# Second block's projections as ten chunk pairs of seven products, weight sums on GpSimd, convolution begun with two chunks

## The chip, the cores and the metric

One core of one Trainium2 chip runs the whole kernel. The metric is the device time of one execution in microseconds; less is better. All data is float32. In the code and the profile TensorE is PE (PEld its weight loads), VectorE is DVE, ScalarE is ACT, GpSimd is POOL and SyncE is SP.

## The reference

The program computes two transformer-like blocks one after the other on 512 tokens of 1024 features. The change touches only the second block, which puts 16 meta tokens ahead (528 tokens) and has two layers. Each layer begins with one wide projection, out of which come queries, keys, values, a gated depthwise convolution and two gates:

```
u = h @ w_in[i]                       # 528 x 1024 times 1024 x 3840
q = u[..., :512]                      # 8 heads of 64
k = u[..., 512:640]                   # 2 heads of 64
v = u[..., 640:768]
y_attn = sliding_window_attention(q, k, v, ...) @ w_attn_proj[i]
y_conv = conformer_conv(u[..., 768:1792], ...) @ w_conv_proj[i]
mix = (sigmoid(u[..., 1792:2816]) * y_attn + sigmoid(u[..., 2816:]) * y_conv) @ w_out[i]

def conformer_conv(u, dw, db, g, b):  # 31 taps, causal, per channel
    val, gate = split(u, 2)
    h = val * sigmoid(gate)
    return silu(layer_norm(depthwise_conv(h, dw) + db, g, b))
```

## The kernel before, in words

The features of a layer lie transposed in `core.feat` (128 partitions x 8 x 528 tokens). The projection's output is made in chunks of 128 output features: 4 of the convolution's value, 4 of its gate, 4 of queries, 2 of keys, 1 of values (token by token, not feature by feature), 16 of gates. The host lays the weights out in that order (`lay_out`). Each key head of 64 features is laid out twice in its chunk, since PE's score matmuls need the key on the same partitions as the query, either 0 to 63 or 64 to 127.

`project_and_attend` (L2351) is one block in which each engine has its own program, in an order written out by hand; semaphores tie them together.

- SP loads the weights in groups of up to four chunks (`GROUPS`, L2108), 2 MB each, alternately into `core.lead` and `w`. Groups 0 and 1 are there before layer 0's stage starts; in layer 1 group 1 is issued at its start. `load_behind(g, semaphore, count)` (L2434) issues group g when the named work has been done.
- PE: a chunk is made in two halves of 264 tokens, each by 8 matmuls into one of two PSUM banks (`ring`), by `chunk_half` (L2460). It makes the 28 halves of value, gate, queries and keys, then the values (L2530), then the first 14 halves of the gates (`EARLY`), and then waits for the convolution (`own`, `CONVOLVED` = 124 instructions). After that come the column sums of the convolution's result (L2481), the scores and the attention, unit by unit, with the other 18 gate halves placed between (two halves directly behind the first scores).
- ACT moves each half out of its bank (`take`, L2563 to L2565), through a sigmoid for the convolution's gate.
- DVE multiplies value and gate (L2648) of all four chunks, then runs the convolution: two iterations, each with 31 taps for two chunks of 528 tokens (L2660 for the first tap, L2663 for the others: source and result in SBUF, the weight a column). Each instruction waits for the one two places before it. Then it centres the result (L2671) once PE has the column sums.
- POOL clears the padding of the gated input (L2450) and then does nothing until the softmax (L2456).

The two layers of the block run this function with the same code; in layer 0 the attention has two small units for the meta tokens more. The dense feed-forward part of layer 0 (`dense_ffn`, L2848) already multiplies in pairs of chunks by seven products (L2947), with the sums on DVE.

Of the kernel before, what the change touches and what calls it, by code (L numbers as in the profile page):

```python
# [2107 lines left out]
GROUPS = [(0, 4), (4, 4), (8, 4), (12, 3), (15, 4), (19, 4), (23, 4), (27, 4)]  # L2108
# [242 lines left out]
def project_and_attend(core, A, i, weights, mix_in):  # L2351


    units = []
# [9 lines left out]
    PLAIN = 14  # L2364
# [3 lines left out]
    first_gate = PLAIN * 2  # L2368
    CONVOLVED = CCK * CW
    with ExitStack() as ctx:  # L2370
# [9 lines left out]
        ring = core.ps(ctx, "ring", [P, RINGS, BANK])  # L2380
        ps = core.ps(ctx, "ps", [P, 2, BANK])
        pm = core.ps(ctx, "pm", [P, 2, BANK])
        ptr = core.ps(ctx, "ptr", [P, BANK])
        po = core.ps(ctx, "po", [P, BANK])
# [3 lines left out]
             "t_out o_made o_out centred squared rooted inverse normed silu").split())  # L2388
        ident, ones = core.cst[:, ID0:ID0 + P], core.cst[:, ONE0:ONE0 + P]
        eps = core.cols2[:, LAYERS * C2L:LAYERS * C2L + 1]  # L2390
        tap0 = i * C2L
        SUMS = first_gate + EARLY
# [11 lines left out]

        def gate_half(h):

            return first_gate + h + (0 if h < EARLY else 2 if h < EARLY + 2 else 4)
# [18 lines left out]
        with core.block() as block:  # L2426

            @block.sync
            def _(sp):
                if i == 0:  # L2430
                    core.tables.load(sp)
                if i:
                    weights.first_loads(sp, (1,))
                def load_behind(g, done, count):  # L2434
                    sp.wait_ge(done, count)
                    weights.load(sp, g % 2, *GROUPS[g])

# [11 lines left out]
            def _(pool):  # L2449
                pool.memset(glu[:, :, 0:CW - 1], 0.0).then_inc(padded, 1)  # L2450
# [8 lines left out]
            def _(pe):  # L2459
                def chunk_half(n, g, c, half, part=None):  # L2460
# [3 lines left out]
                    for k in ks:  # L2464
                        last = pe.matmul(ring[:, n % RINGS, 0:HALF], w[g % 2][:, c, k * P:(k + 1) * P], core.feat[:, k, cols(half)],  # L2465
                                         start=k == 0, stop=k == DK - 1)
# [3 lines left out]
                def gate(h, part=None):  # L2470
                    g, c = 4 + h // 8, h // 2 % 4
                    if h % 8 == 0 and not part:
                        pe.wait_ge(w_landed[g % 2], 16 * (g // 2 + 1))
                    chunk_half(gate_half(h), g, c, h % 2, part)

                def column_sums(n0, src):
                    for half in range(2):
                        n = n0 + half
                        pe.wait_ge(taken, n - RINGS + 1)
# [4 lines left out]
                def scores(u):  # L2484
# [4 lines left out]
                    for j in range(G):  # L2489
# [3 lines left out]
                        last = pe.matmul(meta(u)[:, b, c, :], q, core.k_t[rows, hk, 0:META], start=True, stop=True)  # L2493
                        if width:
                            last = pe.matmul(main(u)[:, b, c, 2 * P - width:], q, core.k_t[rows, hk, lo - width:lo], start=True, stop=True)
# [26 lines left out]
                for g in range(4):  # L2522
                    pe.wait_ge(w_landed[g % 2], 16 * (g // 2 + 1))
                    for c in range(4 if g < 3 else 2):
                        for half in range(2):
                            n = (g * 4 + c) * 2 + half
                            chunk_half(n, g, c, half)
                for t, r in ROWS:
                    for k in range(DK):
                        last = pe.matmul(ps[0:r, t // 4, (t % 4) * P:(t % 4 + 1) * P], core.feat[:, k, row_cols(t)],  # L2530
                                         w[1][:, 2, k * P:(k + 1) * P], start=k == 0, stop=k == DK - 1)
                last.then_inc(v_made, 1)
# [29 lines left out]
            def _(act):  # L2562
                def take(n, dst, f, half):  # L2563
                    act.wait_ge(projected, n + 1)
                    act.activation(dst[:, cols(half)], ring[:, n % RINGS, 0:HALF], f).then_inc(taken, 1)  # L2565

                def gate(h):
                    if h // 2 >= 2 * DK - CCK - 1:
                        act.wait_ge(normed, CCK)
                    take(gate_half(h), core.gates[:, h // 2, :], ACT.Copy, h % 2)  # L2570
# [11 lines left out]
                act.wait_ge(padded, 1)  # L2582
                for n in range(first_gate):
                    c, half = divmod(n, 2)
                    if c < 4:
                        take(n, val[:, c, :], ACT.Copy, half)
                    elif c < 8:
                        take(n, glu[:, c - 4, CW - 1:], ACT.Sigmoid, half)
                    elif c < 12:
                        take(n, core.q_t[:, c - 8, :], ACT.Copy, half)  # L2590
                    else:
                        take(n, core.k_t[:, c - 12, :], ACT.Copy, half)
                act.wait_ge(v_made, 1)
                act.activation(core.v_tok[:, 0:4, :].rearrange("p t c -> p (t c)"), ps[:, 0, :], ACT.Copy)
                act.activation(core.v_tok[0:META, 4, :], ps[0:META, 1, 0:P], ACT.Copy).then_inc(v_out, 1)
                for h in range(EARLY):
                    gate(h)
                act.wait_ge(centred, CCK)
                act.wait_ge(taken, SUMS)
# [1082 lines left out]
def lay_out(inputs):  # L3682
# [7 lines left out]
    ks = [w2[:, :, q1 + h * HD:q1 + (h + 1) * HD] for h in range(KVH)]  # L3690
    w2 = np.concatenate([w2[:, :, v1:v1 + 2 * CC], w2[:, :, 0:q1], ks[0], ks[0], ks[1], ks[1], w2[:, :, k1:v1],
                         w2[:, :, v1 + 2 * CC:]], axis=2)
# [67 lines left out]
```

## Time and profile before

| | us |
|---|---|
| median of 3 runs (lowest, highest) | 3172.27 (3168.92, 3183.77) |
| the profiled execution's own time | 3173.29 |
| its span | 3171.5 |
| PE busy | 2946.1 (93%) |
| DVE busy | 1131.1 (36%) |
| ACT busy | 567.5 (18%) |
| POOL busy | 221.1 (7%) |
| mean granted clock of PE, of full speed | 0.961 |

The span is the time from the first to the last instruction in one profiled execution. Busy times of engines overlap, so they do not add up to the span. A matmul's record (its mean is printed in ns) is longer than the distance between two matmuls, since they are pipelined; the rate of a stretch is best read from two starts with the number of records between them. Each matmul of the code on float32 data is two records.

### The profile page before, as it was taken

The numbers are of one execution on the slowest core, as the hardware profiler recorded it, in microseconds if no ns is written. First come the engines' busy times: TensorE is split into PE (matmuls) and PEld (weight loads), VectorE is DVE, ScalarE is ACT, GpSimd is POOL, SyncE is SP. The second block draws the span as 40 slices with busy tenths as digits, with TensorE's granted clock in tenths as the row PEclk, the third lists the DMA queues.
The fourth block names the chain that finished last, engine by engine and source line by source line (L and its number), as shares of the span: only waits on it lengthen the run. The fifth ranks groups of instructions, "written<-read, shape, count | busy, mean of one in ns | idle before, by whom it ended". The sixth has DMA issues, their size and how long they took to land. (4 is left out here: it accounts for less than half of the span.)

```text
span 3171.5 us, 43527 instructions
## 1 busy us (share of the span) xinstructions
PE 2946.1 (93%) x18242; PEld 1809.0 (57%) x18242; DVE 1131.1 (36%) x2071; ACT 567.5 (18%) x1340; POOL 221.1 (7%) x204
## 2 busy tenths in 40 slices
PE   8998799999969979999999999999999799999897
PEld 4544788654433327876668874478775444444343
DVE  5666666563132132922343320229212211111014
ACT  3232333222111121134011110011340000000001
POOL 0000332340000000001100000000110100000001
PEclk9999799999969988999999999999999799999998
DMA  3411000107089942212032212022020724547917
GB/s 117 103 59 44 3 17 17 54 14 277 32 339 430 423 200 64 76 58 80 41 126 80 88 71 87 0 73 103 31 95 1 278 74 181 235 181 322 416 44 290
DMA packets 79329, 414.20 MB, mean 131 GB/s; under 512 B 10515, under 2 KB 16019, under 8 KB 63428
## 3 DMA queue, kind: packets, MB, share of 16 engines
q1 hardware_dynamic: 67868, 384.75, 30.6%
q10 hardware_dynamic: 7848, 14.61, 1.9%
q0 software_dynamic: 3456, 12.58, 1.1%
q8 instruction: 118, 1.93, 0.3%
q14 instruction: 39, 0.32, 0.0%
HBM read 383.17 MB, written 28.76 MB: 130 GB/s over the span
## 5 line engine op out<-in xcount | busy, mean ns | idle before, releaser
L3469 PE MATMUL pgu<-gu,xg 128*64 128x320 f32 (+1 forms) x2560 | 393.8, 463 | 10.3 <-POOLq L3397 10.3
L3469 PEld LDWEIGHTS pgu<-gu,xg 128*64 128x64 f32 x2560 | 182.4, 137 | 206.3 <-issue 131.6
L312 PE MATMUL proj<-feat,w 128*128 128x512 f32 x576 | 256.1, 598 | 2.5 <-PEq L153 2.5
L2465 PE MATMUL ring<-feat,lead 128*128 128x264 f32 x1024 | 242.6, 397 | 3.0 <-PEq L3069 1.5
L2465 PEld LDWEIGHTS ring<-feat,lead 128*128 128x128 f32 x1024 | 197.6, 196 | 40.4 <-issue 6.3
L2465 PE MATMUL ring<-feat,w 128*128 128x264 f32 x896 | 209.4, 390 | 0.0
L3476 PE MATMUL py<-down,hm_t 128*64 128x512 f32 x880 | 199.0, 600 | 10.4 <-POOLq L3397 10.4
L2465 PEld LDWEIGHTS ring<-feat,w 128*128 128x128 f32 x896 | 169.1, 192 | 30.3 <-issue 2.4
L312 PEld LDWEIGHTS proj<-feat,w 128*128 128x128 f32 x576 | 107.3, 191 | 124.8 <-issue 124.8
L497 DVE SCALAR_TENSOR_TENSOR mixed<-padded,taps,mixed 128x512 f32<-128x512 f32 x216 | 162.4, 752 | 7.7
L2663 DVE SCALAR_TENSOR_TENSOR conv<-vg,cols,conv x240 | 163.4, 769 | 0.0
L3089 PE MATMUL po<-wd,hm 128*128 128x512 f32 x352 | 152.2, 593 | 0.0
L3538 DVE TENSOR_TENSOR hm<-sg,pgu 128x384 f32<-128x384 f32 (+1 forms) x40 | 20.8, 521 | 314.9 <-PE pgu L3469 209.5
L3476 PEld LDWEIGHTS py<-down,hm_t 128*64 128x64 f32 x880 | 61.7, 138 | 121.0 <-issue 103.8
L3089 PEld LDWEIGHTS po<-wd,hm 128*128 128x128 f32 x352 | 66.5, 190 | 83.5 <-issue 83.5
L2778 PE MATMUL pp<-wo,feat 128*128 128x512 f32 x256 | 111.3, 593 | 2.8 <-POOL feat L2827 2.8
L3421 ACT ACT_TABLE_LOAD x19 | 24.4, 1283 | 459.7 <-PE pgu L3469 280.9
L3035 DVE TENSOR_TENSOR gb<-gb,pp 128x264 f32<-128x264 f32 x66 | 28.2, 429 | 174.8 <-PE pp L2947 174.8
L2778 PEld LDWEIGHTS pp<-wo,feat 128*128 128x128 f32 x256 | 48.1, 190 | 61.9 <-issue 61.9
L2947 PE MATMUL pp<-sums_x,sums_w 128*128 128x264 f32 x352 | 80.1, 386 | 0.0
L2947 PEld LDWEIGHTS pp<-sums_x,sums_w 128*128 128x128 f32 x352 | 66.9, 190 | 11.4
L2219 ACT ACTIVATE rt<-rt 128x1 f32<-128x1 f32 (+1 forms) x15 | 3.0, 203 | 376.7 <-DVE rt L2189 376.7
(521 smaller groups left out, 3952.1 us busy)
## 6 DMA issues: line engine op xcount, KB each, us to landing
gu<-in_moe_gu SPq DMA_DIRECT2D x16, 3072.0 KB, 13.5
gu<-in_moe_gu SPq DMA_DIRECT2D x16, 2560.0 KB, 15.9
ring<-in_w_gate SPq DMA_DIRECT2D x16, 2048.0 KB, 13.6
ring<-in_w_up SPq DMA_DIRECT2D x16, 2048.0 KB, 15.2
ring<-in_w_down SPq DMA_DIRECT2D x16, 2048.0 KB, 17.5
w<-in_w_in SPq DMA_DIRECT2D x15, 2048.0 KB, 7.8
down<-in_moe_down SPq DMA_DIRECT2D x8, 3072.0 KB
down<-in_moe_down SPq DMA_DIRECT2D x8, 2560.0 KB, 20.8
```

Of the source, the lines that this page charges most:

```text
L312: last = pe.matmul(proj[:, n % 2, :], w[:, g % 2, k, c * P:(c + 1) * P], core.feat[:, k, :], start=k == 0, stop=k == DK - 1)
L497: dve.scalar_tensor_tensor(out=out, in0=src[:, j:j + SEQ], scalar=taps[:, n, j:j + 1], in1=out, op0=ALU.mult, op1=ALU.add).then_inc(convol ...
L2465: last = pe.matmul(ring[:, n % RINGS, 0:HALF], w[g % 2][:, c, k * P:(k + 1) * P], core.feat[:, k, cols(half)], start=k == 0, stop=k == DK - 1)
L2663: dve.scalar_tensor_tensor(out=out, in0=src[:, j:j + NTOK], scalar=tap(c, j), in1=out, op0=ALU.mult, op1=ALU.add).then_inc(own, 1)
L2778: last = pe.matmul(pp[:, n % 2, n // 2 % 2, 0, :], mixed[:, k, row_cols(t)], wo[:, k, half * BANK:(half + 1) * BANK], start=k == 0, stop=k ...
L2947: last = pe.matmul(bank, lhs[:, a, k * P:(k + 1) * P], rhs[:, k, :], start=begin and k == 0, stop=k == KH - 1, skip_group_check=True)
L3035: dve.tensor_tensor(dst, dst, bank, ALU.add).then_inc(added, 1)
L3089: last = pe.matmul(po[:, t, :], hm[:, f, row_cols(t)], wd[half][:, f, :], start=f == 0, stop=f == FC - 1)
L3421: act.activation(sg[:, q, 0:n], pgu[:, 2 * q, 0:n], ACT.Silu).then_inc(silu, 1)
L3469: last = pe.matmul(pgu[half(h), part, 0:n], xg[:, k, :], w[:, k, h, :], start=k == 0, stop=k == DK - 1)
L3476: last = pe.matmul(py[half(h), :], hm_t[:, c, :], down[:, c, h * BANK:(h + 1) * BANK], start=c == 0, stop=c == XC - 1)
L3538: dve.tensor_tensor(hm[:, c0:c0 + n], sg[:, q, 0:n], pgu[:, 2 * q + 1, 0:n], ALU.mult).then_inc(multiplied, 1)
```

## The change

Strassen's method, in the form of seven products, is used on pairs of chunks. A pair's output (2 x 128 features by 2 x 264 tokens) is a 2 x 2 block product: weights of the two chunks and two halves of the 1024 input features, times the two halves of the features and of the tokens. Instead of 8 products of 4 matmuls each it takes 7, with sums of weight blocks (four per pair, on POOL) and of feature blocks (four per layer, on DVE). The products accumulate in three PSUM banks a pair; ACT copies each bank out before the next product goes onto it, some of them into tiles where they are kept, and POOL adds the kept ones to the result (three adds of 264 columns a pair). The ten pairs are: value 0 and 1, gate 0 and 1, value 2 and 3, gate 2 and 3 (of the convolution), two pairs of queries, one pair of the keys with the first chunk of the gates, and three pairs of gates. The keys take one chunk instead of two; PE swaps its two halves of 64 partitions by an identity matmul for the second copy. The values follow pair 6. The 14 early gate halves of before are now in the pairs; the other 18 stay where they were, in layer 1 without the meta tokens (256 columns instead of 264). DVE begins the convolution of chunks 0 and 1 as soon as these two are there, and does the gating of each iteration at its start. The loads stand behind the pairs.

```diff
-GROUPS = [(0, 4), (4, 4), (8, 4), (12, 3), (15, 4), (19, 4), (23, 4), (27, 4)]
+GROUPS = [(0, 4), (4, 4), (8, 4), (12, 3), (15, 4), (19, 4), (23, 4), (27, 3)]
...
+    KH = DK // 2
+    (P1, P2, P6, P5, P7, P3, P4) = range(7)
+    PRODUCTS = 7
+    ADDED = 3
+    PAIR_AT = [(0, 0), (1, 0), (0, 2), (1, 2), (2, 0), (2, 2), (3, 0), (4, 0), (4, 2), (5, 0)]
+    PAIRS2 = len(PAIR_AT)
+    GLU_PAIRS = (1, 3)
+    KEY_PAIR = 6
...
+        def gate_cols(half):
+            return slice(META + half * (SEQ // 2), META + (half + 1) * (SEQ // 2)) if i else cols(half)
...
-                load_behind(2, projected, 8)
-                load_behind(3, projected, 16)
-                load_behind(4, projected, 24)
+                load_behind(2, product, 3 * PRODUCTS)
+                load_behind(3, product, 4 * PRODUCTS)
+                load_behind(4, product, 6 * PRODUCTS)
                 load_behind(5, v_made, 1)
-                load_behind(6, projected, gate_half(7) + 1)
+                load_behind(6, product, 9 * PRODUCTS)
...
-                load_behind(7, projected, gate_half(15) + 1)
+                load_behind(7, projected, gate_half(17) + 1)
 
             @block.gpsimd
             def _(pool):
+                def sum_weights(r):
+                    g, c = PAIR_AT[r]
+                    pool.wait_ge(w_landed[g % 2], 16 * (g // 2 + 1))
+                    if r >= 2:
+                        pool.wait_ge(product, PRODUCTS * (r - 2) + P3 + 1)
+                    for n, (out, x, y, f) in enumerate(((s1(r), weight(r, 1, 0), weight(r, 1, 1), ALU.add),
+                                                        (s2(r), s1(r), weight(r, 0, 0), ALU.subtract),
+                                                        (s3(r), weight(r, 0, 0), weight(r, 1, 0), ALU.subtract),
+                                                        (s4(r), weight(r, 0, 1), s2(r), ALU.subtract))):
+                        if n:
+                            pool.wait_ge(w_summed, 4 * r + n)
+                        pool.tensor_tensor(out, x, y, f).then_inc(w_summed, 1)
+
+                def add(r, dst, n, have):
+                    pool.wait_ge(copied, PRODUCTS * r + have + 1)
+                    pool.tensor_tensor(dst, dst, kept(r, n), ALU.add).then_inc(added, 1)
+
+                sum_weights(0)
                 pool.memset(glu[:, :, 0:CW - 1], 0.0).then_inc(padded, 1)
+                sum_weights(1)
                 core.clear_retired(pool)
+                for r in range(PAIRS2):
+                    add(r, row(r, 0)[:, 0:HALF], 0, P2)
+                    add(r, row(r, 1)[:, HALF:], 2, P7)
+                    add(r, row(r, 0)[:, HALF:], 1, P3)
+                    if r + 2 < PAIRS2:
+                        sum_weights(r + 2)
...
+                def multiply(r, bank, lhs, rhs, begin):
+                    for k in range(KH):
+                        last = pe.matmul(bank, lhs[:, k * P:(k + 1) * P], rhs[:, k, :], start=begin and k == 0,
+                                         stop=k == KH - 1, skip_group_check=True)
+                    last.then_inc(product, 1)
+
+                def pair(r):
+                    g, c = PAIR_AT[r]
+                    pe.wait_ge(w_landed[g % 2], 16 * (g // 2 + 1))
+                    if r >= 2:
+                        pe.wait_ge(copied, PRODUCTS * (r - 2) + P4 + 1)
+                    multiply(r, bank_x(r), weight(r, 0, 0), x11, True)
+                    multiply(r, bank_y(r), weight(r, 0, 1), x21, True)
+                    pe.wait_ge(w_summed, 4 * r + 2)
+                    pe.wait_ge(x_summed, 2)
+                    pe.wait_ge(copied, PRODUCTS * r + P1 + 1)
+                    multiply(r, bank_x(r), s2(r), t2, False)
+                    multiply(r, bank_z(r), s1(r), t1, True)
+                    pe.wait_ge(w_summed, 4 * r + 4)
+                    pe.wait_ge(x_summed, 4)
+                    pe.wait_ge(copied, PRODUCTS * r + P6 + 1)
+                    multiply(r, bank_x(r), s3(r), t3, False)
+                    pe.wait_ge(copied, PRODUCTS * r + P5 + 1)
+                    multiply(r, bank_z(r), s4(r), x22, False)
+                    pe.wait_ge(copied, PRODUCTS * r + P7 + 1)
+                    multiply(r, bank_x(r), weight(r, 1, 1), t4, False)
...
+                def swap_keys():
+                    pe.wait_ge(added, ADDED * (KEY_PAIR + 1))
+                    for half, bank in enumerate((bank_y(PAIRS2), bank_z(PAIRS2))):
+                        for b in range(2):
+                            last = pe.matmul(bank[b * HD:(b + 1) * HD, :], ident[:, (1 - b) * HD:(2 - b) * HD],
+                                             core.k_t[:, 0, cols(half)], start=True, stop=True)
+                        last.then_inc(swapped, 1)
...
-                for h in range(EARLY):
-                    gate(h)
+                for r in range(PAIRS2):
+                    pair(r)
+                    if r == KEY_PAIR:
+                        values()
+                swap_keys()
                 pe.wait_ge(own, CONVOLVED)
                 column_sums(SUMS, core.conv)
                 pe.wait_ge(v_out, 1)
+                pe.wait_ge(k_out, 2)
                 scores(0)
...
+                def open_sums(r):
+                    act.wait_ge(added, ADDED * (r + 1))
+                    act.activation(row(r, 0), row(r, 0), ACT.Sigmoid).then_inc(opened, 1)
+                    act.activation(row(r, 1)[:, HALF:], row(r, 1)[:, HALF:], ACT.Sigmoid).then_inc(opened, 1)
+
+                def pair(r):
+                    if r >= 2:
+                        act.wait_ge(added, ADDED * (r - 1))
+                    copy(r, P1, kept(r, 0), bank_x(r))
+                    copy(r, P2, row(r, 0)[:, 0:HALF], bank_y(r))
+                    copy(r, P6, kept(r, 1), bank_x(r))
+                    copy(r, P5, kept(r, 2), bank_z(r))
+                    if r - 1 in GLU_PAIRS:
+                        open_sums(r - 1)
+                    copy(r, P7, row(r, 1)[:, HALF:], bank_x(r))
+                    copy(r, P3, row(r, 0)[:, HALF:], bank_z(r))
+                    copy(r, P4, row(r, 1)[:, 0:HALF], bank_x(r), ACT.Sigmoid if r in GLU_PAIRS else ACT.Copy)
...
             @block.vector
             def _(dve):
-                for c in range(CCK):
-                    dve.wait_ge(taken, 2 * (4 + c) + 2)
-                    g = glu[:, c, CW - 1:]
-                    dve.tensor_tensor(g, g, val[:, c, :], ALU.mult).then_inc(gated, 1)
-                dve.wait_ge(gated, CCK)
+                for n, (out, x, y) in enumerate(((t1, x12, x11), (t2, x22, t1), (t3, x22, x12), (t4, x21, t2))):
+                    if n:
+                        dve.wait_ge(x_summed, n)
+                    dve.tensor_tensor(out, x, y, ALU.subtract).then_inc(x_summed, 1)
+                dve.wait_ge(padded, 1)
                 if i == 0:
                     dve.wait_ge(core.tables.columns_in, 16)
                 with dve.Fori(0, CCK // 2) as r:
                     done = r * (2 * CW)
+                    dve.wait_ge(opened, r * 2 + 2)
+                    for e in range(2):
+                        c = r * 2 + e
+                        g = glu[:, bass.ds(c, 1), CW - 1:].rearrange("p a n -> p (a n)")
+                        v = val[:, bass.ds(c, 1), :].rearrange("p a n -> p (a n)")
+                        dve.tensor_tensor(g, g, v, ALU.mult).then_inc(gated, 1)
+                    dve.wait_ge(gated, r * 2 + 2)
                     for j in range(CW):
```

## Rows read from the trace of the kernel before

**Rows 1.** The page's first part: busy time, share and instructions of each engine.

```profile
PE 2946.1 (93%) x18242; PEld 1809.0 (57%) x18242; DVE 1131.1 (36%) x2071; ACT 567.5 (18%) x1340; POOL 221.1 (7%) x204
```

**Rows 2.** Instructions in order of time, layer 0, PE: start, us, work, count.

```profile
1201.22 31.53 PE L2465 MATMUL ring<-feat,lead 128*128 128x264 f32 x128 [1.48 <-PEq L2253]
1232.58 28.64 PE L2465 MATMUL ring<-feat,w 128*128 128x264 f32 x128
1261.06 28.64 PE L2465 MATMUL ring<-feat,lead 128*128 128x264 f32 x128
...
1303.78 9.16 PE L2530 MATMUL ps<-w,feat 128*128 128x128 f32 x80
...
1362.81 3.72 PE L2481 MATMUL ring<-conv,cst 128*128 128x264 f32 x16
```

**Rows 3.** The same for layer 1.

```profile
2068.57 31.34 PE L2465 MATMUL ring<-feat,lead 128*128 128x264 f32 x128 [1.48 <-PEq L3069]
...
2229.98 3.72 PE L2481 MATMUL ring<-conv,cst 128*128 128x264 f32 x16
```

**Rows 4.** Busy time by stretch of 20 us: PE, PEld, DVE, ACT, POOL, granted clock, DMA.

```profile
1201.00:1221.00 20.00, 19.78 (x76) 16.51 (x77) 0.00 (x0) 1.56 (x4) 0.20 (x1) 0.85 0.27 68
```

**Rows 5.** Instructions in order of time, layer 0, DVE.

```profile
1261.68 0.71 DVE L2648 TENSOR_TENSOR vg<-vg 128x528 f32<-128x528 f32 x1 [6.41 <-ACT vg L2565]
1262.92 1.02 DVE L2660 TENSOR_SCALAR conv<-vg,cols  x2 [0.53 <-DVE vg L2648]
...
1304.71 1.02 DVE L2660 TENSOR_SCALAR conv<-vg,cols  x2
1305.64 40.84 DVE L2663 SCALAR_TENSOR_TENSOR conv<-vg,cols,conv  x60
1364.88 1.45 DVE L2671 SCALAR_TENSOR_TENSOR conv<-ring,conv 128x264 f32<-128x264 f32 x4 [18.39 <-PE ring L2481]
```

**Rows 6.** Groups of instructions by line and form, ACT: count, busy us, mean ns.

```profile
L2565 ACT ACTIVATE vg<-ring 128x264 f32<-128x264 f32 x32 | 12.5, 391 | 106.3 <-PE ring L2465 106.3
L2789 ACT ACTIVATE gates<-gates 128x528 f32<-128x528 f32 x16 | 8.6, 628 | 0.0
```

**Rows 7.** DMA issues from 2040 to 2260: KB each, us to landing; SP's first.

```profile
w<-in_w_in SPq DMA_DIRECT2D x3, 2048.0 KB, 7.8
```

**Rows 8.** Groups by line and form, POOL.

```profile
L2827 POOL TENSOR_TENSOR feat<-gates 128x528 f32<-128x528 f32 x8 | 10.4, 1300 | 62.9 <-DVE gates L2803 62.9
L2827 POOL TENSOR_TENSOR feat<-gates 128x512 f32<-128x512 f32 x8 | 10.1, 1267 | 61.4 <-DVE gates L2803 61.4
```

**Rows 9.** In order of time, first block: DVE alone, DVE beside POOL, POOL then, POOL alone.

```profile
597.83 1.29 DVE L1568 TENSOR_TENSOR steps_and_weighted<-cst,scal 128x512 f32<-128x512 f32 x2
...
672.18 2.97 DVE L1568 TENSOR_TENSOR steps_and_weighted<-cst,scal 128x512 f32<-128x512 f32 x2
...
668.77 5.83 POOL L1321 TENSOR_TENSOR steps_and_weighted<-tok_x,scal 128x512 f32<-128x512 f32 x4
...
656.62 1.04 POOL L1328 TENSOR_TENSOR state<-state,scal 128x512 f32<-128x512 f32 x1
```

**Rows 10.** DVE and POOL together earlier, and L1027's durations (min/median/max).

```profile
322.51 4.42 DVE L1027 TENSOR_TENSOR uc<-am,shapes 32x256 f32<-32x256 f32 x4
...
322.56 1.51 POOL L678 TENSOR_TENSOR qm<-qm,chan 128x512 f32<-128x512 f32 x1
...
L1027 DVE TENSOR_TENSOR uc<-am,shapes x32: 403/423/1404, 322.5 to 530.3; 32x256 f32<-32x256 f32 x32
```

**Rows 11.** DVE with an input in PSUM, beside a POOL instruction.

```profile
656.01 0.68 DVE L1599 TENSOR_TENSOR hid<-pi,scal 128x512 f32<-128x512 f32 x1
...
655.38 1.28 POOL L1337 TENSOR_TENSOR chan<-chan,hid 128x512 f32<-128x512 f32 x1 [0.59 <-issue]
```

**Rows 12.** PE in order of time: the same work behind a wait and without one.

```profile
2260.19 2.17 PE L2518 MATMUL po<-pt,v_tok 16*64 16x256 f32 x8 [4.41 <-ACT pt L2627]
...
1404.14 1.23 PE L2518 MATMUL po<-pt,v_tok 16*64 16x256 f32 x8
```

More of the change, by code:

```diff
@@ L2363, in project_and_attend @@
     scale = HD ** -0.5
-    PLAIN = 14
     RINGS = 2
@@ L2388, in project_and_attend @@
              "t_out o_made o_out centred squared rooted inverse normed silu").split())
+        product, copied, added, opened, w_summed, x_summed, swapped, k_out = (
+            core.sem(x) for x in "product copied added opened w_summed x_summed swapped k_out".split())
+        x11, x12 = core.feat[:, 0:KH, 0:HALF], core.feat[:, 0:KH, HALF:]
+        x21, x22 = core.feat[:, KH:, 0:HALF], core.feat[:, KH:, HALF:]
+        t1, t2, t3, t4 = (sums_x[:, n, :, :] for n in range(4))
         ident, ones = core.cst[:, ID0:ID0 + P], core.cst[:, ONE0:ONE0 + P]
@@ new lines, in values @@
+                def values():
+                    for t, r in ROWS:
+                        for k in range(DK):
+                            last = pe.matmul(ps[0:r, t // 4, (t % 4) * P:(t % 4 + 1) * P], core.feat[:, k, row_cols(t)],
+                                             w[1][:, 2, k * P:(k + 1) * P], start=k == 0, stop=k == DK - 1)
+                    last.then_inc(v_made, 1)
+                def swap_keys():
[5 more added lines that the diff above has]
+                        last.then_inc(swapped, 1)
@@ L2464, in chunk_half @@
                     for k in ks:
-                        last = pe.matmul(ring[:, n % RINGS, 0:HALF], w[g % 2][:, c, k * P:(k + 1) * P], core.feat[:, k, cols(half)],
+                        src = core.feat[:, k, gate_cols(half)]
+                        last = pe.matmul(ring[:, n % RINGS, 0:src.shape[1]], w[g % 2][:, c, k * P:(k + 1) * P], src,
                                          start=k == 0, stop=k == DK - 1)
@@ L2470, in gate @@
                 def gate(h, part=None):
-                    g, c = 4 + h // 8, h // 2 % 4
-                    if h % 8 == 0 and not part:
+                    g, c = gate_at(h)
+                    if c == 0 and h % 2 == 0 and not part:
                         pe.wait_ge(w_landed[g % 2], 16 * (g // 2 + 1))
@@ L2478, in column_sums @@
                         n = n0 + half
-                        pe.wait_ge(taken, n - RINGS + 1)
+                        if n >= RINGS:
+                            pe.wait_ge(taken, n - RINGS + 1)
+                        elif half:
+                            pe.wait_ge(copied, PRODUCTS * PAIRS2)
                         for c in range(CCK):
@@ L2492, in scores @@
                         q = core.q_t[rows, hk * 2 + c, q0:q0 + nq]
-                        last = pe.matmul(meta(u)[:, b, c, :], q, core.k_t[rows, hk, 0:META], start=True, stop=True)
+                        last = pe.matmul(meta(u)[:, b, c, :], q, core.k_t[rows, abs(b - hk), 0:META], start=True, stop=True)
                         if width:
-                            last = pe.matmul(main(u)[:, b, c, 2 * P - width:], q, core.k_t[rows, hk, lo - width:lo], start=True, stop=True)
+                            last = pe.matmul(main(u)[:, b, c, 2 * P - width:], q, core.k_t[rows, abs(b - hk), lo - width:lo], start=True, stop=True)
                     last.then_inc(s_made, 1)
@@ L2562, in _, with copy @@
             def _(act):
-                def take(n, dst, f, half):
-                    act.wait_ge(projected, n + 1)
-                    act.activation(dst[:, cols(half)], ring[:, n % RINGS, 0:HALF], f).then_inc(taken, 1)
+                def copy(r, j, dst, bank, f=ACT.Copy):
+                    act.wait_ge(product, PRODUCTS * r + j + 1)
+                    act.activation(dst, bank, f).then_inc(copied, 1)
+                def open_sums(r):
[14 more added lines that the diff above has]
+                    copy(r, P4, row(r, 1)[:, 0:HALF], bank_x(r), ACT.Sigmoid if r in GLU_PAIRS else ACT.Copy)
                 def gate(h):
@@ L2569, in gate @@
                         act.wait_ge(normed, CCK)
-                    take(gate_half(h), core.gates[:, h // 2, :], ACT.Copy, h % 2)
+                    n = gate_half(h)
+                    dst = core.gates[:, h // 2, gate_cols(h % 2)]
+                    act.wait_ge(projected, n + 1)
+                    act.activation(dst, ring[:, n % RINGS, 0:dst.shape[1]], ACT.Copy).then_inc(taken, 1)
                 def soft(u):
@@ L2580, in soft @@
                     act.activation(x[:, 1, :], x[:, 1, :], ACT.Exp).then_inc(exped, 1)
[L2582 to L2597, printed above, removed]
+                for r in range(PAIRS2):
+                    pair(r)
+                    if r == KEY_PAIR:
+                        act.wait_ge(v_made, 1)
+                        act.activation(core.v_tok[:, 0:4, :].rearrange("p t c -> p (t c)"), ps[:, 0, :], ACT.Copy)
+                        act.activation(core.v_tok[0:META, 4, :], ps[0:META, 1, 0:P], ACT.Copy).then_inc(v_out, 1)
+                for half, bank in enumerate((bank_y(PAIRS2), bank_z(PAIRS2))):
+                    act.wait_ge(swapped, half + 1)
+                    act.activation(core.k_t[:, 1, cols(half)], bank, ACT.Copy).then_inc(k_out, 1)
                 act.wait_ge(centred, CCK)
-                act.wait_ge(taken, SUMS)
                 act.sem_inc(taken, 1)
```

57 lines of the change are left out of this document (35 added, 22 removed).

## The prediction

> **What bounds the kernel now.** I read the page first: TensorE (PE) is busy 93% of the span, so anything that takes matmuls away looks like gain [rows 1]. That share is an average; the change touches two stages, the projections of the two layers of the second block, so I then read PE in order of time there [rows 2]. In layer 0 the stage starts at 1201.22 and runs without a gap (28 ring halves, the values, 14 gate halves) to the column sums at 1362.81: 161.6 us. I call the start T=0. Layer 1 is a copy: 2068.57 to 2229.98, 161.4 us [rows 3]. In steady state 128 records of 128x264 take 28.48 us from start to start, 0.2225 us each (each matmul of the code is two records); the first 128 take 31.36, that is 2.9 us more, with a granted clock of 0.85 in the first 20 us [rows 2, 4]. The values cost 9.1 us.
>
> The column sums wait for the convolution on VectorE (DVE), the chain of 124 dependent instructions, so I read DVE in the same stretch [rows 5]. Four gatings come as the ring gives them, the convolution starts at 1262.92 (T=61.7), each of its two iterations takes 41.8 us (1262.92 to 1304.71), and it ends at 1346.5, T=145.3. Then DVE is idle 18.4 us until PE's column sums. So PE sets the end now, and the convolution has 16.3 us of slack. Two paths run side by side: what the change is worth is the later of the two afterwards.
>
> **PE's path.** Before the sums: 336 matmuls of ring halves (42 x 8) and the values. After: 10 pairs x 7 products x 4 = 280, the values, and 4 for the swapped keys. In records: 560 x 0.2225 = 124.6, plus 9.1, plus 8 x 0.2225 = 1.8, plus the 2.9 of the slow start: PE arrives at T=138.5 instead of 161.6, 23.1 us earlier. The parts I cost at nothing on it: ScalarE's copies, 0.39 us each [rows 6], lie under the next product of 8 x 0.2225 = 1.8 us, since each bank is reused only one product later; where the two sigmoids (0.63 for 528 columns and 0.39 for 264) come between two copies, the copy of P7 ends about 1.3 us late, still under P3. The one load of an activation table falls on the last copy of pair 1, which PE needs only a pair later. Weight loads land in 7.8 us [rows 7]; the tightest is group 2, issued behind pair 2 and needed a pair (12.46 us) later; layer 1's group 1 is issued at its start (2068.5, SyncE is free then) and its sums are needed at about T=19. SyncE's queue has only the layer-0 tables and these loads in it. The last group is issued behind gate half 17 instead of 15 and used from half 26 instead of 24. The DVE sums of the inputs (four of 1056 elements, estimated at 1.3 us each from 0.71 for 528 [rows 5]) must be half done at about T=6.5 and all done at T=10: close, up to 1 us.
>
> **GpSimd (POOL).** Per pair, 4 sums of 128x512 and 3 adds of 128x264. An addition with two full inputs takes 1.27 us for 512 and 1.30 for 528 [rows 8]; by that slope (2.06 ns an element) 264 take 0.76. That is 7.4 us of 12.46 per pair: POOL keeps up, and even if each instruction is held up by 0.35 us (half a DVE instruction) it has 2.5 us left. It works one pair ahead, so PE waits for no sum. In POOL's queue the sums of pair 4 stand ahead of the adds of pair 3; with the load landing at T=48.1 they end near 54.5, and the adds are through at 57.8, before pair 4's sigmoids need them at about 60.
>
> **The convolution's path.** Pairs 0 and 1 end at T=27.8; after P1, P2, P6 and P5 of pair 2 (7.1 us) and a copy the two sigmoids run, and DVE starts at T=36.6. A gating and the step to the convolution cost 1.24 us and a second gating 0.71, 1.95 together; an iteration 41.8; the second iteration's inputs are long there: 36.6 + 2 x 43.75 = T 124.1, if nothing slows DVE. That would be 14 us before PE.
>
> But before the change POOL is silent here, and now it reads and writes SBUF all the time. In the first block the trace has this pair of engines side by side. While POOL runs four additions back to back (5.83 us for 4), DVE's additions with both inputs in SBUF take 2.97 us for two; two of the same line without POOL take 1.29 [rows 9]. So in steady alternation one DVE and one POOL instruction share 1.45 us: DVE loses 0.8 us for each POOL instruction, which alone takes 1.04 (its second input is broadcast). Where POOL's two inputs are full, as here, four DVE instructions of 32x256 take 4.42 us, 1.1 each, where the median is 0.42 and the largest is 1.40: a loss of up to 0.98 for each POOL instruction, whose own records grow from 1.27 to 1.51 [rows 10]. A DVE instruction with one input in PSUM is not slowed beside POOL (0.68) [rows 11]. The convolution's instruction reads its source and its accumulator from SBUF, so it is of the first kind; that scalar_tensor_tensor behaves like tensor_tensor is my choice, no row shows it.
>
> Nearest to the new case are the full inputs of [rows 10]. I take 0.95 us for a sum and 0.48 for an add (half the elements). Under the convolution lie the sums of pairs 4 to 9 (24) and the last 2 adds of pair 2 with those of pairs 3 to 9 (23): 22.8 + 11.0 = 33.8 us. The convolution ends at T=157.9, and the column sums start at 158.1 instead of 161.6. Ends of this cost: nothing at all; the smallest slot that the trace shows, 0.7 and 0.35 (25 us); POOL's whole record each time, 1.28 and 0.76 (48.2 us).
>
> The Trainium skill (page "SBUF — State Buffer", section "Who interferes with whom") says that a DVE instruction with two SBUF inputs contends with a GpSimd instruction that reads SBUF, and that whoever comes second waits for the whole instruction. That speaks against this change. The trace agrees on which instructions collide, but an alternation takes 1.45 us where the whole-instruction reading gives 0.64 + 1.02 = 1.66; by the page's wording the sum would be that of the second rival.
>
> PE then stands idle from T=138.5 to 158.1. After such a gap it is slow: behind 4.4 us of waiting the row of 8 records at 2260.19 takes 2.17 us instead of 1.23 [rows 12], and the start of the stage costs 2.9 us. I take 2.9 again. What follows the sums (scores, 18 gate halves, attention) is unchanged, except that in layer 1 the gate halves have 256 columns for 264: 288 records x 0.2225 x 8/264 = 1.9 us less.
>
> **Sum.** Per layer 158.1 + 2.9 - 161.6 = -0.6 us; two layers -1.2; gates -1.9: -3.1 us. The profiled execution took 3173.29 (span 3171.5), so 3170.2 by its time; the median of the three runs is 3172.27, 1.0 lower, which gives 3169.
>
> **Rivals.**
> 1. DVE loses little, because the dependent chain leaves POOL room between instructions (0.681 us apart where two free additions come 0.60 to 0.65 apart). With no loss PE sets the end at T=138.5: 2 x 23.1 + 1.9 = 48 us less, 3124. With the small slots (25 us lost) the convolution ends at 149.1: 2 x 9.4 + 1.9 = 21 less, 3152. For it: no row shows this form of instruction beside POOL. Against it: every DVE row with two SBUF inputs beside POOL is slowed.
> 2. Slower: POOL's whole record blocks DVE each time. Loss 48.2, convolution ends at T=172.3: 2 x (172.5 + 2.9 - 161.6) - 1.9 = +26, 3198. It decides from a loss of about 35 us a layer on (break even), and is over 0.5% slower from 43.3. For it: the 1.40 of [rows 10], where a 0.42 instruction lost 0.98. Against it: the 1.45 of the alternation.
> 3. POOL falls behind: were each of its instructions to wait a whole DVE instruction (0.68), it would need 4 x 2.0 + 3 x 1.5 = 12.7 us a pair against PE's 12.46. PE would arrive up to 2 us later, hidden behind the convolution: 3169 again.
>
> **How the numbers follow.** Forecast 0.56, with a range of its own of 3157 to 3184 (a loss of 28 to 41 us a layer); rival 1 0.26; rival 2 0.14; rival 3 0.04. A measurement of this kernel can tell 0.5%, 16 us. Faster by more than that needs a loss below 27.4 us: rival 1 and the edge of the forecast, 0.28. Slower: rival 2, 0.14. The rest, 0.58, is no change. The range takes in most of rival 1 and half the way to rival 2: 3136 to 3188.
>
> **What would show it.** In the changed trace: PE's last product before the values and after pair 9 near T=137, then a gap of some 20 us before the column sums, ended by DVE's convolution; the mean of the convolution's instruction well above 0.769 us, its two iterations 55 to 60 us instead of 41.8; POOL's sums at 1.4 to 1.6 us instead of 1.27; a granted clock under 1 at the column sums. I am wrong if the convolution's instruction stays near 0.77 and the column sums follow PE's last product without a gap, or if the gap is over 28 us, or if PE waits inside the pairs for sums or copies.

## The result and the profile after

The changed kernel takes 3196.85 us (median of 7, 3193.4 to 3198.0) where the kernel before takes 3169.1 (median of 7 beside it, 3165.65 to 3183.77). The medians stand 27.8 us apart; the ratio taken over the executions is 1.0073, with a 95% interval of 1.0061 to 1.0085. It is slower by 0.7%, clear of the noise. The forecast was 3169, no change. T counts from PE's first matmul of the stage, and everything is set against the rows of before.

The busy times of the page after, and PE in order of time: layer 0, then layer 1.

```profile
PE 2908.3 (91%) x18034; PEld 1772.3 (55%) x18034; DVE 1192.7 (37%) x2079; ACT 593.3 (19%) x1408; POOL 454.0 (14%) x344
```

```profile
1199.55 5.41 PE L2542 MATMUL pp<-feat,lead 128*128 128x264 f32 x16 [1.48 <-PEq L2253]
...
1251.53 3.72 PE L2542 MATMUL pp<-feat,lead 128*128 128x264 f32 x16
1282.26 6.72 PE L2542 MATMUL pp<-sums_x,sums_w 128*128 128x264 f32 x16 [27.01 <-POOL sums_w L2516]
...
1344.17 6.48 PE L2542 MATMUL pp<-sums_x,sums_w 128*128 128x264 f32 x16 [12.18 <-POOL sums_w L2516]
...
1381.89 3.83 PE L2607 MATMUL pp<-conv,cst 128*128 128x264 f32 x16
...
2091.64 6.49 PE L2542 MATMUL pp<-feat,lead 128*128 128x264 f32 x16 [1.48 <-PEq L3208]
...
2228.55 1.11 PE L2578 MATMUL pp<-k_t,cst 128*64 128x264 f32 x8
2250.02 5.83 PE L2607 MATMUL pp<-conv,cst 128*128 128x264 f32 x16 [20.35 <-DVE conv L2802]
```

The two layers run the same code and went two ways. In layer 1 PE has made its swapped keys and is at the wait at T=138.0 (2250.02 - 20.35 - 2091.64), and waits 20.35 us for DVE; the column sums start at T=158.4, where before they started at 161.4 [rows 3]. In layer 0 PE waits inside the pairs, 27.01 us in pair 4 and 12.18 in pair 7, both times for POOL's sums, and the column sums start at T=182.3 instead of 161.6 [rows 2]. To the first matmul of the mixing behind it (1510.92 after, 1489.66 before), layer 0 grew by 22.9 us, counted from PE's start; layer 1 (2370.29, 2348.47) shrank by 1.3. The span grew by 23.7 us, 21.6 of it in these two stretches.

POOL in order of time, layer 0 and layer 1:

```profile
1247.04 33.83 POOL L2516 TENSOR_TENSOR sums_w<-lead 128x512 f32<-128x512 f32 x1 [8.34 <-DMA lead<-in_w_in]
1280.94 1.26 POOL L2516 TENSOR_TENSOR sums_w<-sums_w,lead 128x512 f32<-128x512 f32 x1
...
1315.88 26.90 POOL L2516 TENSOR_TENSOR sums_w<-lead 128x512 f32<-128x512 f32 x1 [9.43 <-DMA lead<-in_w_in]
...
2139.64 5.71 POOL L2516 TENSOR_TENSOR sums_w<-lead 128x512 f32<-128x512 f32 x1 [8.21 <-DMA lead<-in_w_in]
2145.43 1.62 POOL L2516 TENSOR_TENSOR sums_w<-sums_w,lead 128x512 f32<-128x512 f32 x1
2147.13 1.61 POOL L2516 TENSOR_TENSOR lead<-lead 128x512 f32<-128x512 f32 x1
```

and DVE in the same stretches (the rows of 60 are the taps of one iteration):

```profile
1237.45 1.54 DVE L2799 TENSOR_SCALAR conv<-vg,cols  x2 [0.68 <-DVE vg L2791]
1238.91 40.83 DVE L2802 SCALAR_TENSOR_TENSOR conv<-vg,cols,conv  x60
1290.50 2.48 DVE L2791 TENSOR_TENSOR vg<-vg  x2 [10.75 <-ACT vg L2689]
...
1294.76 46.90 DVE L2802 SCALAR_TENSOR_TENSOR conv<-vg,cols,conv  x60
...
2129.80 1.03 DVE L2799 TENSOR_SCALAR conv<-vg,cols  x2 [0.32 <-DVE vg L2791]
2130.76 67.89 DVE L2802 SCALAR_TENSOR_TENSOR conv<-vg,cols,conv  x60
...
2201.61 48.36 DVE L2802 SCALAR_TENSOR_TENSOR conv<-vg,cols,conv  x60
```

One addition of 128x512, 1.27 us before [rows 8], has a record of 33.83 us; I call such an instruction held. It ends 1.1 us behind the end of the first iteration (1238.91 + 40.83 = 1279.74), and that iteration runs at its old speed of 40.83 us [rows 5] as if POOL were not there. Between the iterations POOL comes in; in the second one the next first sum behind a load is held for 26.90 us, until 1342.78, again 1.1 us behind the chain's end (1294.76 + 46.90). In layer 1 the addition is held for 5.71 us, and from then on POOL and DVE take turns, so that the iteration takes 67.89 us.

Behind such waits PE is slow: granted clock 0.53 in the wait of pair 4 and 0.50, the level of 1.2 GHz, in the 6 us after it (per stretch: PE, PEld, DVE, ACT, POOL, clock, DMA). The 16 records behind the two waits take 6.72 and 6.48 us, where others of the same form take 3.72.

```profile
1256.00:1282.00 26.00, 0.00 (x0) 0.00 (x0) 23.74 (x35) 0.00 (x0) 25.92 (x2) 0.53 0.06 26
1282.00:1288.00 6.00, 5.74 (x13) 4.51 (x14) 0.00 (x0) 0.39 (x1) 5.84 (x7) 0.50 0.00 0
```

### The profile page after: what moved, and what is told of

It reads as the page before. It is cut to its first block and busy times, and to the rows that moved or that the text cites. A ratio compares the mean times of both kernels' runs of the same rounds, so it can differ in the third digit from the quotient of the medians.

```text
span 3195.2 us, 43423 instructions
## 1 busy us (share of the span) xinstructions
PE 2908.3 (91%) x18034; PEld 1772.3 (55%) x18034; DVE 1192.7 (37%) x2079; ACT 593.3 (19%) x1408; POOL 454.0 (14%) x344
## 5 line engine op out<-in xcount | busy, mean ns | idle before, releaser
L3608 PEld LDWEIGHTS pgu<-gu,xg 128*64 128x64 f32 x2560 | 182.3, 137 | 206.3 <-issue 131.8
L2802 DVE SCALAR_TENSOR_TENSOR conv<-vg,cols,conv x240 | 204.0, 925 | 0.0
L2516 POOL TENSOR_TENSOR sums_w<-lead 128x512 f32<-128x512 f32 x12 | 78.9, 6573 | 693.0 <-POOLq L3208 520.8
L2542 PE MATMUL pp<-sums_x,sums_w 128*128 128x264 f32 x320 | 80.2, 407 | 39.2 <-POOL sums_w L2516 39.2
L3545 POOL DMA_INDIRECT gu<-moe_out,place x8 | 8.1, 1016 | 641.7 <-POOLq L3541 639.6
L2588 PE MATMUL pp<-feat,w 128*128 128x264 f32 (+1 forms) x320 | 80.6, 401 | 0.0
L3086 PE MATMUL pp<-sums_x,sums_w 128*128 128x264 f32 x352 | 80.1, 386 | 0.0
```

The costliest lines, as they stand in the source:

```text
L2516: pool.tensor_tensor(out, x, y, f).then_inc(w_summed, 1)
L2542: last = pe.matmul(bank, lhs[:, k * P:(k + 1) * P], rhs[:, k, :], start=begin and k == 0, stop=k == KH - 1, skip_group_check=True)
L2588: last = pe.matmul(ring[:, n % RINGS, 0:src.shape[1]], w[g % 2][:, c, k * P:(k + 1) * P], src, start=k == 0, stop=k == DK - 1)
L2802: dve.scalar_tensor_tensor(out=out, in0=src[:, j:j + NTOK], scalar=tap(c, j), in1=out, op0=ALU.mult, op1=ALU.add).then_inc(own, 1)
L3086: last = pe.matmul(bank, lhs[:, a, k * P:(k + 1) * P], rhs[:, k, :], start=begin and k == 0, stop=k == KH - 1, skip_group_check=True)
L3608: last = pe.matmul(pgu[half(h), part, 0:n], xg[:, k, :], w[:, k, h, :], start=k == 0, stop=k == DK - 1)
```

## The experiments

Theory A: a chain of DVE instructions with no gap keeps a port to SBUF that it shares with POOL; a POOL instruction that needs this port and comes when the chain has run undisturbed for a while waits until the chain breaks. Rival B: the long records wait for the weight load in front of them (the rows of both name a DMA). Rival C: POOL's own long pause makes it slow. The runs show which instructions are held beside which; that a port is the reason is the theory's part.

**The chain by itself.** This is no part of the kernel: 40 dependent instructions like the convolution's a trial, and one piece of POOL work after a set number of them (steps). In a chain two apart, as the convolution is, each instruction waits for the one two places before it; one apart, for the one directly before it.

```diff
+ dve.wait_ge(own, at + (j - apart + 1))
+ dve.scalar_tensor_tensor(out=out, in0=src[:, j:j + W], scalar=one[:, j:j + 1], in1=out, ...).then_inc(own, 1)
...
+ pool.wait_ge(own, start + s)
+ pool.tensor_tensor(wo[:, 0, 0:size], wa[:, 0:size], wb[:, 0:size], ALU.add).then_inc(done, 1)
```

> Not the kernel: DVE's convolution chain by itself (40 dependent instructions of 128x528 a trial, each waiting for the one two places before), and in each trial one POOL instruction that comes after 4 to 20 steps of the chain; POOL has been idle until then, or busy with memsets; it is an addition of 512 or 264 elements, a copy or a memset. Then six trials with the chain one apart and six with it four apart. Theory A (a chain in undisturbed rhythm keeps the shared SBUF port; an addition that comes after a long calm waits for the chain's end): additions that come after 8 or more calm steps last until the chain ends (10 to 20 us), those after 4 to 6 steps about 1.2 to 1.8 us; memsets 0.5 us at any place; with the chain one apart, where a gap lies between two instructions, none is over 2 us. Rival B (the long instructions of layer 0 waited for the weight load, not for the port): no instruction here is over 2 us, since there is no load. Rival C (a long idle time makes POOL slow, not DVE's rhythm): the additions with memsets ahead of them are short, those without are long at the same step.

POOL's records, in order: an addition after 6 steps; 12 memsets and the addition behind them, at step 12; a copy after 12; a memset after 12; an addition after 5; and with the chain one apart an addition after 8 and four after 20.

```profile
38.58 24.13 POOL L73 TENSOR_TENSOR wo<-wa,wb 128x512 f32<-128x512 f32 x1 [27.56 <-DVE acc L94]
...
201.95 6.92 POOL L61 MEMSET wm<- 128x512 f32 x12 [0.82 <-DVE acc L91]
208.84 19.98 POOL L73 TENSOR_TENSOR wo<-wa,wb 128x512 f32<-128x512 f32 x1
...
345.83 19.43 POOL L69 COPY wo<-wa 128x512 f32<-128x512 f32 x1 [7.61 <-DVE acc L94]
...
399.88 0.52 POOL L71 MEMSET wo<- 128x512 f32 x1 [7.60 <-DVE acc L94]
...
512.37 1.72 POOL L73 TENSOR_TENSOR wo<-wa,wb 128x512 f32<-128x512 f32 x1 [2.87 <-DVE acc L94]
...
654.15 1.26 POOL L73 TENSOR_TENSOR wo<-wa,wb 128x512 f32<-128x512 f32 x1 [6.00 <-DVE acc L94]
...
828.78 6.31 POOL L73 TENSOR_TENSOR wo<-wa,wb 128x512 f32<-128x512 f32 x4 [38.27 <-DVE acc L94]
```

All 10 lone additions of 512 that came after 6 to 20 steps lasted to the end of the chain, 14.62 to 24.13 us, also those of 264 after 12 and 20 (19.54, 14.10) and the copies; those after 4 and 5 steps took 1.72. Additions are held with no load in the program, so B is not needed; 12 memsets directly ahead change nothing (19.98 where an idle POOL had 20.06), so C is refuted; no memset was held. With the chain one apart nothing is held; four apart it is held as two apart (22.77). I had expected an addition after 6 steps to be short, and it was held.

> The chain by itself again, POOL idle before one addition of 512 elements a trial. 14 trials come after 2 to 8 steps, each twice: by the first such run (1.7 us after 4 and 5 steps, 24 us after 6) the additions after up to 5 steps take under 2 us and those after 6 or more last to the chain's end, both times. Then chains of another kind, with the addition after 10, 13, 17 and 20 steps. Chain of instructions with one input in SBUF: if the shared read port is what is kept, none is over 2 us; if any dense chain shuts POOL out, they last 14 to 20 us. Chain of tensor_tensor with two inputs: held like the convolution's. A gap every 8 steps: the addition waits at most 8 x 0.68 = 5.4 us and takes at most 7; a gap every 16 steps: at most 10.9 + 1.3 = 12.2 us.

The edit is in the list of trials, `s` from 2 to 8 and the forms of the chain. POOL's records: after 5 steps, after 6, a chain of instructions with one SBUF input, a gap every 8 steps, a gap every 16.

```profile
93.73 1.72 POOL L61 TENSOR_TENSOR wo<-wa,wb 128x512 f32<-128x512 f32 x1 [26.88 <-DVE acc L87]
122.33 24.13 POOL L61 TENSOR_TENSOR wo<-wa,wb 128x512 f32<-128x512 f32 x1 [26.88 <-DVE acc L87]
...
401.11 14.99 POOL L61 TENSOR_TENSOR wo<-wa,wb 128x512 f32<-128x512 f32 x1 [4.56 <-DVE acc L82]
...
582.70 1.72 POOL L61 TENSOR_TENSOR wo<-wa,wb 128x512 f32<-128x512 f32 x1 [6.39 <-DVE acc L87]
...
696.37 5.12 POOL L61 TENSOR_TENSOR wo<-wa,wb 128x512 f32<-128x512 f32 x1 [19.79 <-DVE acc L87]
```

Both passes give the same: up to 5 instructions since the chain's start 1.72 us, from 6 on held to the end. A gap every 8 leaves 1.72 in all four trials, one every 16 gives 5.12, 3.08, 1.72, 1.72. A chain of tensor_scalar from SBUF to SBUF holds POOL too (14.99 to 10.34 us), like one of tensor_tensor (19.61 to 13.42). So a second SBUF tensor as input is not needed. But this form steps every 0.47 us where tensor_tensor steps every 0.62, so it may read in another way, and the trial does not tell which port is kept. Why the sixth instruction decides here is open too, and it is no rule for the kernel: with four pairs (below), an add of 264 elements that came 4.6 us behind POOL's last turn, with seven of the convolution's instructions started between, took 0.96 us.

**Sums as memsets.** It leaves out POOL's sums and adds and puts memsets in their place, so the block's values are meaningless and only the projection stages are read.

```diff
-                        pool.tensor_tensor(out, x, y, f).then_inc(w_summed, 1)
+                        write_only(w_summed, idle[:, 0:2 * BANK])
-                    pool.tensor_tensor(dst, dst, kept(r, n), ALU.add).then_inc(added, 1)
+                    write_only(added, idle[:, 0:2 * HALF])
```

> POOL's sums of weights and its adds are left out and memsets of 1024 and 528 elements stand in their place (write only, about 0.95 and 0.5 us), every wait kept; the second block computes something else, so only its projection stages are read, not its total. Theory A (port): no POOL instruction over 1.2 us, both iterations of the convolution 41.8 to 42.5 us in both layers, PE has no wait inside the pairs, and the column sums start at T = 138 to 141 in both layers (182.3 and 158.4 in the changed kernel). Rival B (late load): one POOL instruction behind each load of group 2 and 4 in layer 0 is still 27 to 34 us, and PE waits as long; column sums in layer 0 at T = 165 or more.

POOL behind the load of group 2, the first iteration, and PE's column sums in layer 0:

```profile
1246.83 10.75 POOL L2513 MEMSET pt<- 128x1024 f32 x12 [8.82 <-DMA lead<-in_w_in]
```

```profile
1238.22 40.83 DVE L2815 SCALAR_TENSOR_TENSOR conv<-vg,cols,conv  x60
...
1281.63 40.83 DVE L2815 SCALAR_TENSOR_TENSOR conv<-vg,cols,conv  x60
```

```profile
1336.15 3.83 PE L2620 MATMUL pp<-conv,cst 128*128 128x264 f32 x16
```

The load lands at the same place, nothing is held, both iterations keep 40.83 us, and PE's column sums start 136.5 us after its start at 1199.70, a little ahead of the 138 to 141 expected. So the load does not hold POOL, and layer 0's loss comes from POOL instructions that read SBUF.

**A gap at every fourth tap.**

```diff
-                                dve.wait_ge(own, done + (2 * j + e - 1))
+                                dve.wait_ge(own, done + (2 * j + e - (0 if j % 4 == 0 and e == 0 else 1)))
```

> One edit: at every fourth tap the first of the two chunks' instructions waits for the one directly before it, so that a gap of about 0.1 us stands in the chain 7 times an iteration. Theory A (port kept by the rhythm): a POOL addition waits for at most the next gap, so none is over 7 us; layer 0 becomes like layer 1: column sums at T = 156 to 163 in both (182.3 and 158.4 without the edit), total 20 to 28 us below the changed kernel: 3167 to 3177. An iteration without POOL would take about 43 us. Rival B (late load): POOL's long instructions stay at 27 to 34 us and the total at 3195 or above.

POOL's first sum behind the load, and PE in layer 0, which started at 1197.39. The gap that the edit makes measures 0.18 us:

```profile
1245.52 1.91 POOL L2516 TENSOR_TENSOR sums_w<-lead 128x512 f32<-128x512 f32 x1 [8.61 <-DMA lead<-in_w_in]
```

```profile
1357.60 6.34 PE L2607 MATMUL pp<-conv,cst 128*128 128x264 f32 x16 [22.71 <-DVE conv L2802]
```

33.83 us became 1.91, no single POOL instruction of the stage takes over 2.2 us, the column sums are at T=160.2 and in layer 1 at 160.5: 3175.43 us, ratio 1.001 (1.000 to 1.0019). One changed term in one wait takes away 21 us, and leaves what the prediction described: no gain.

**Seven products in fewer pairs.** A pair outside them is 32 plain matmuls. First four pairs, those ahead of the convolution:

```diff
+                    if r < STRASSEN:
+                        pair(r)
+                    else:
+                        plain(r)
```

> Only the four pairs before the convolution begins (value and gate) are made by seven products; the other six pairs are made by 32 plain matmuls each, the keys still projected once, the convolution still begun with two chunks. POOL then has only adds of pairs 2 and 3 beside the convolution. Theory A: PE's path is 138.5 + 6 x 1.78 = T 149.2, the convolution ends at T = 124 to 128 (iterations of 42 to 44 us), so PE sets the end again: column sums at T = 149 to 150 in both layers, 12 us below before per layer, total 3142 to 3148. Rival B (loads late): long waits in layer 0 stay, total above 3160. Rival D (the seven products themselves are slower on PE than plain ones, by the waits for copies): column sums after T = 153.

```profile
1346.86 3.83 PE L2626 MATMUL pp<-conv,cst 128*128 128x264 f32 x16
```

T=148.5 from 1198.32, iterations of 42.12 and 40.83 us: 3146.36 us, ratio 0.9919 (0.9899 to 0.9938).

> All ten pairs by 32 plain matmuls, no sums on POOL or DVE; the keys are still projected once and swapped, the convolution still begins with two chunks, and layer 1's late gate halves still have 256 columns. It is what the change is worth without Strassen. Theory: PE's path is T = 155 to 156.5, the convolution runs at 41.8 us an iteration and ends near T = 121; per layer 5 to 6 us below before, with the 1.9 us of the gates 12 to 14 us: 3157 to 3161 against 3172.6. If the early convolution by itself were worth something, the time would be lower still; it should not be, since PE sets the end before and after.

3160.57 us, ratio 0.9959 (0.9945 to 0.9973), column sums at T=155.5 in both layers: making the keys once and 256 columns are worth 12 us without any seven products. The early convolution is in it too, but PE sets the end before and after.

> Seven products in pairs 0 to 5, plain matmuls in pairs 6 to 9, and the gap at every fourth tap. Beside the convolution POOL has 8 sums and 11 adds. Theory A with the prices of the prediction (0.95 and 0.48 us of DVE's time each): the convolution ends at T = 139 and PE arrives at T = 145, so PE sets the end: 16.6 us a layer below before, total 3135 to 3140. If a sum costs DVE 1.3 us or more, the convolution ends after PE and the total is above 3142. No POOL addition over 7 us.

> The same with seven products in pairs 0 to 6. PE arrives at T = 143; POOL has 12 sums and 14 adds beside the convolution, which by the prices 0.95 and 0.48 ends at T = 144 to 145: the two paths are level, 17 us a layer below before, total 3134 to 3140, within 3 us of the six pairs. At 1.3 us a sum the convolution ends at T = 149 and this kernel is 8 us slower than the one with six.

Column sums in layer 0 with six and with seven pairs:

```profile
1348.10 3.83 PE L2626 MATMUL pp<-conv,cst 128*128 128x264 f32 x16
```

```profile
1345.29 3.83 PE L2626 MATMUL pp<-conv,cst 128*128 128x264 f32 x16 [1.80 <-DVE conv L2842]
```

Six pairs with gaps: 3140.38 us, ratio 0.989 (0.9869 to 0.9911), PE without a wait. Seven: 3142.19, ratio 0.9896 (0.9876 to 0.9917), PE waits 1.80 us for the convolution: the two paths are level, and the prices hold. The column sums start at T=144.8 and 145.1. Both totals lie up to 2 us above the ranges expected, and between the two the runs show no difference. Both beat the kernel before and the changed one.

> Seven products in 6 pairs without the gaps: it tells what the gaps are worth. Theory A: the sums of pair 4 come behind a load and after a calm of the chain, so the first is held until the iteration ends near T = 82 in layer 0, PE waits about 25 us in pair 4 and arrives near T = 172; POOL is then free of the second iteration, so the convolution ends near T = 127. Column sums at T = 168 to 175 in a layer where nothing breaks the chain: total 3160 to 3195, at least 20 us above the same kernel with gaps (3140.4). If the gaps did nothing, the total is within 5 us of 3140.

```profile
1284.45 5.82 PE L2545 MATMUL pp<-sums_x,sums_w 128*128 128x264 f32 x16 [27.01 <-POOL sums_w L2517]
...
1375.19 3.83 PE L2626 MATMUL pp<-conv,cst 128*128 128x264 f32 x16
```

3167.84 us, ratio 0.9984 (0.9974 to 0.9995): without the gaps the wait of pair 4 is back and 27 us are lost. Nearly all of it is layer 0, with column sums at T=174.1 instead of 144.8; in layer 1, where the addition is held for only 5.64 us, they start at 145.2 and 144.9.

> The changed kernel with one part undone: DVE begins the convolution only when all four gated chunks are there. Theory A: it begins near T = 62 instead of 37, POOL's sums of pairs 4 and 5 are then done without it, but the sums behind the loads of groups 3 and 4 come after a calm of the chain and are held for tens of us; PE waits for them, column sums at T = 172 or later, total 3195 to 3225. If the early beginning is worth nothing, the total stays at 3196 or falls by what POOL gains from a free port, to 3180 to 3190.

```diff
-                    dve.wait_ge(opened, r * 2 + 2)
+                    dve.wait_ge(opened, CCK)
```

PE, layer 1:

```profile
2195.80 5.41 PE L2542 MATMUL pp<-sums_x,sums_w 128*128 128x264 f32 x16 [11.94 <-POOL sums_w L2516]
```

3199.4 us in two executions, ratio 1.0081 (1.0056 to 1.0106). It is not told apart from the changed kernel. The chain begins later, at T=63 in layer 0, and POOL is held once in each layer, for 26.9 and 27.9 us. PE's column sums start at T=172.1 in layer 0 and 171.9 in layer 1.

## Why the prediction was wrong

- PE's path was right: T=138.5 forecast, 138.0 in layer 1, where no POOL instruction holds PE. So was the beginning of the convolution, T=38.6 forecast for its first tap, 38.2 measured.
- The price of sharing was right. In steady turns a sum's records stand 1.70 us apart (2145.43, 2147.13) where the chain alone steps 0.68: DVE loses 1.0 us, forecast 0.95. Layer 1's iterations take 68.8 and 49.8 us instead of 41.8, a loss of 35.0, forecast 33.8. The convolution ends there at T=158.3, forecast 157.9; the wait is 20.35 us, forecast 19.6. The slow matmuls behind the wait were put at 2.9 us and cost 2.0 (5.83 us for 16 records instead of 3.83).
- The step that failed stands under GpSimd: "It works one pair ahead, so PE waits for no sum", with "the sums of pair 4 ... end near 54.5". They ended at T=85.3. I took the turns of [rows 9, 10] for what always happens. In those rows both engines were at work when they met. Here POOL comes after 8 to 9 us of waiting for a load into a chain that has run undisturbed, and it is not served once while some 48 DVE instructions pass. PE then waited 27.01 and 12.18 us inside the pairs and ran slow behind both waits, 3.0 and 2.8 us more than usual. Layer 0 lost 22.9 us by that instead of gaining 0.6.
- Rival 2 gave 3198 and the time is 3196.9, but not by its mechanism: it priced every POOL instruction at its whole record, and two instructions did it. Rival 3 had the place (PE waits for sums), and a size of 2 us (its sum, 4 x 2.0 + 3 x 1.5, is 12.5 and not 12.7, so hardly over PE's 12.46). Its claim that such a wait hides behind the convolution fails: while POOL is held DVE runs at its old speed, the convolution of layer 0 was through at T=142.1, and PE came 40 us behind it.
- The rule of the Trainium skill that I weighed (page "SBUF — State Buffer", sections "Who interferes with whom" and "SBUF: two separate sides": the second waits for the whole instruction) names the right pair of instructions, but one DVE instruction is 0.76 us and the wait was 33.83.
- Nothing in the prediction tells layer 1 from layer 0. In layer 1 POOL got its turn at 2144.1, in the middle of the iteration. What broke the chain there is not isolated, but the trace has a lead: DVE's own register instruction ahead of the convolution's next one is 0.35 us late (single records of the trace: it follows its forerunner by 0.52 us instead of 0.16), so the next one starts 0.01 us behind it, where the others of that wait start 0.36 us behind theirs. In the run with gaps such lateness shows as a longer gap:

```profile
2129.98 11.46 DVE L2802 SCALAR_TENSOR_TENSOR conv<-vg,cols,conv  x8 [0.53 <-DVE conv L2802]
```

With six pairs and no gaps the 5.64 us ended at the same instruction of layer 1's chain, with the same lateness. Where the convolution waits for four chunks, one as late (the instruction at 1294.66) ended nothing, so lateness alone does not explain it.

## What to carry to other kernels

Before giving work to GpSimd, look at what VectorE does beside it: a dense chain of SBUF instructions can shut it out until the chain breaks, 33.83 us here, even if the same two engines take turns elsewhere in the trace. Either keep such work out of the chain's time (4 pairs) or leave the chain a gap every 8 instructions (6 pairs with gaps), and stop moving work when the two paths are level. Where one engine is relieved, compute the other paths to the same wait first: here 23 us of matmuls bought nothing as long as 34 us of POOL's turns lay on the other path.

## What the runs showed of the hardware

- In the chain by itself a POOL addition of 512 elements that comes after up to 5 instructions takes 1.72 us; from 6 on, with the instructions two or four apart and no gap, an addition or a copy lasted to the chain's end in every trial, up to 24.13 us. In the kernel adds of 264 that came up to 4.6 us behind POOL's last turn still took about 1 us. A chain in which each instruction waits for the one directly before it held no POOL instruction (1.26 us). A gap of 0.18 us every 8 instructions turned 33.83 us into 1.91.
- A held POOL addition costs DVE about as much as a served one: 40 steps take 26.8 us beside a memset, 27.6 with one held and 27.8 with one served after 5 steps.
- A tensor_scalar chain from SBUF to SBUF shuts POOL out as well (up to 14.99 us); no POOL memset was held (0.52 us).
